# Quarter sums of feed-forward weights: on VectorE, or added in flight by transfers

## What is computed

```python
def _conv_ffn(h, w_up, conv_w, conv_b, w_down):
    up = h @ w_up
    ...
    up = lax.conv_general_dilated(up, rhs, window_strides=(1,), padding=[(CONV_WIDTH - 1, 0)],
                                  dimension_numbers=('NWC', 'WIO', 'NWC'),
                                  feature_group_count=C) + conv_b
    gate, val = up[..., :D_FF], up[..., D_FF:]
    return (jax.nn.silu(gate) * val) @ w_down
```

## Time and profile before

| | us |
|---|---|
| time, median of 3 runs | 1533.74 (1533.73 to 1533.94) |
| profiled execution, its own time | 1533.46 |
| span of the profiled execution | 1531.6 |
| TensorE busy | 1485.4 |
| VectorE busy | 544.0 |
| ScalarE busy | 341.4 |
| GpSimd busy (issuing) | 22.3 |

### The profile page before, as it was taken

How to read it: one execution, slowest core, us unless ns; L and a number is a source line. 1 busy time by engine, 2 the same in 40 slices (tenths; PEclk the granted TensorE clock), 3 DMA queues, 4 the chain that set the end, 5 groups by cost and what they waited for, 6 DMA issues and landing times.

```text
span 1531.6 us, 19436 instructions
## 1 busy us (share of the span) xinstructions
PE 1485.4 (97%) x7522; PEld 841.1 (55%) x7522; DVE 544.0 (36%) x1058; ACT 341.4 (22%) x720; POOL 22.3 (1%) x43
## 2 busy tenths in 40 slices
PE   9999999999999999999989899999989999999997
PEld 8667888999997765444423334433324443433332
DVE  3665665888862343421211121211110212121112
ACT  2443142222223452211101111111101111110112
POOL 0000000000000000000000000000000000000000
PEclk9999999999999999999999999999999999999999
DMA  9735654566652264999999999999999999999996
GB/s 377 290 110 222 248 196 146 214 246 247 268 225 59 79 272 174 391 429 426 430 427 429 429 418 426 428 429 427 429 426 429 413 428 428 426 428 426 427 428 264
DMA packets 46727, 513.61 MB, mean 335 GB/s; under 512 B 5264, under 2 KB 5408, under 8 KB 8384
## 3 DMA queue, kind: packets, MB, share of 16 engines
q1 hardware_dynamic: 41984, 482.53, 76.4%
q0 software_dynamic: 4672, 30.06, 5.1%
HBM read 511.51 MB, written 1.06 MB: 335 GB/s over the span
## 4 chain that ended last, share of the span: by engine, by line
PE 80%; DMA 15%; DVE 2%; ACT 1%; issue 1%; SPq 0%; DVEq 0%; ACTq 0%
PE bank L1452 32%; PE bank L796 13%; DMA ring<-in_gate_w 13%; PE bank L1061 8%; PE bank L1099 5%; PE bank L1416 3%; PE bank L1577 3%; PE bank L1484 3%; PE bank L1300 2%; PE bank L907 2%; DMA ring<-in_down_w 2%; PE bank L1469 2%; PE bank L1253 1%; PE bank L1242 1%; PE bank L1193 1%
## 5 line engine op out<-in xcount | busy, mean ns | idle before, releaser
L1452 PE MATMUL bank<-ring,probs_slab 128*64 128x512 f32 x2824 | 630.6, 596 | 26.6 <-DMA ring<-in_gate_w 15.3
L1452 PEld LDWEIGHTS bank<-ring,probs_slab 128*64 128x64 f32 x2824 | 195.3, 137 | 413.7 <-issue 373.3
L2754 DVE TENSOR_TENSOR squares<-bank,tab 128x512 f32<-128x512 f32 x31 | 21.4, 692 | 465.2 <-PE bank L1469 465.2
L2762 DVE TENSOR_TENSOR squares<-bank,tab 128x512 f32<-128x512 f32 x31 | 21.4, 691 | 180.0 <-PE bank L1469 180.0
L796 PE MATMUL bank<-normed,ring 128*128 128x256 f32 x384 | 84.7, 381 | 0.4 <-ACT normed L1742 0.4
L796 PEld LDWEIGHTS bank<-normed,ring 128*128 128x128 f32 x384 | 72.2, 190 | 11.9 <-ACT normed L1742 1.2
L1099 PE MATMUL bank<-big_slab,ring 128*128 128x256 f32 x352 | 77.6, 380 | 0.0
L1099 PEld LDWEIGHTS bank<-big_slab,ring 128*128 128x128 f32 x352 | 66.3, 191 | 8.4
L2097 ACT ACTIVATE squares<-bank 128x512 f32<-128x512 f32 x31 | 18.5, 597 | 228.1 <-PE bank L1452 228.1
L1416 PEld LDWEIGHTS bank<-tab,residual 128*128 128x128 f32 x512 | 58.4, 192 | 12.9 <-issue 12.9
L2107 ACT ACTIVATE squares<-bank 128x512 f32<-128x512 f32 x30 | 17.9, 597 | 202.4 <-PE bank L1452 202.4
(11 more groups left out here) (426 smaller groups left out, 1612.8 us busy)
## 6 DMA issues: line engine op xcount, KB each, us to landing
ring<-in_down_w SPq DMA_DIRECT2D x61, 2048.0 KB, 17.8
ring<-in_up_w SPq DMA_DIRECT2D x60, 2048.0 KB, 19.5
ring<-in_gate_w SPq DMA_DIRECT2D x58, 2048.0 KB, 19.3
ring<-in_front_w SPq DMA_DIRECT2D x72, 1024.0 KB, 5.0
memory_slab<-in_mod_w POOLq DMA_DIRECT2D x10, 1024.0 KB, 6.6
cross_keys_slab<-in_mod_w POOLq DMA_DIRECT2D x5, 1024.0 KB, 7.9
probs_turned_slab<-in_mod_w POOLq DMA_DIRECT2D x5, 1024.0 KB, 6.9
ring<-in_down_w SPq DMA_DIRECT2D x5, 1024.0 KB, 22.9
```

The source lines that it names most:

```text
L1452: mm = pe.matmul(to[half * SLOTS:(half + 1) * SLOTS, :], tokens(k), weights[:, half * D + i * HALF:half * D + (i + 1) * HALF], start=(k == ...
```

## The change

- t1 and the sum in the ring's slot are no longer formed by VectorE. GpSimd issues three transfers per chunk, each of a quarter (128 x 512, 256 KB) from `front_w` in HBM: a plain copy of quarter (0, 0) into t1, quarter (1, 1) added in flight onto quarter (0, 1) in the ring's slot, and, when the copy has landed, quarter (0, 1) added in flight onto t1. `add_quarters` waits for the products of chunk f - 2 and for the transfers of chunk f - 1 before it begins.
- VectorE forms t2 and t4 alone, after waiting for t1 (`row_sum_here`). Signs differ, since the transfers only add; the merge gets one instruction more (its last one, 128 x 256, becomes two of 128 x 128), and two of the token sums change sign.
- TensorE waits in addition for the sum in the ring's slot (`column_sum_here`).
- On GpSimd's queue the transfers of chunks 2 and 3 stand ahead of `load_mod` 8 to 10. The later `load_mod` are placed after `add_quarters(f + 2)` of the step in which `modulate(n - 3)` is done. They still wait for it.
- Two pairs of semaphores are joined (the two gain rows; the final root), and counts are adapted.

```diff
-WEIGHT_SUMS, MERGES, INPUT_SUMS, _n = {2: 0, 3: 8}, {}, 4, 12
+WEIGHT_SUMS, MERGES, INPUT_SUMS, _n = {2: 0, 3: 6}, {}, 2, 8
...
-            for n in range(DC, MOD_ROUNDS * DC):
+            def late_mod(n):
                 pool.wait_ge(s_mod, mod_steps(max(n - 2, DC)))
                 load_mod(n)
+
+            def add_quarters(f):
+
+                i = SEVEN.index(f)
+                w, slot, here = ff_ring(f)
+                q = f if f < 2 else 2 + 3 * (f // 2 - 1) + f % 2
+                part = lambda k_half, half: weight_part(front_w[FF_FIRST + q], k_half, half)
+                t1 = ff_b[i % 2][0]
+                if i >= 2:
+                    pool.wait_ge(s_ff_up, SEVEN[i - 2] + 1)
+                else:
+                    pool.wait_ge(s_mod, mod_steps(DC))
+                if i:
+                    pool.wait_ge(row_sum_here, 32 * i)
+                    pool.wait_ge(column_sum_here, 16 * i)
+                pool.dma_start(t1, part(0, 0)).then_inc(row_sum_here, 16)
+                pool.wait_ge(chunk_here[slot], here)
+                pool.dma_start(weight_part(w, 0, 1), part(1, 1), accum_op=ADD).then_inc(column_sum_here, 16)
+                pool.wait_ge(row_sum_here, 32 * i + 16)
+                pool.dma_start(t1, part(0, 1), accum_op=ADD).then_inc(row_sum_here, 16)
+
+            add_quarters(2)
+            add_quarters(3)
+            for n in (DC, DC + 1, DC + 2):
+                late_mod(n)
+            used_at = {n: f for f, group in MODULATED_AT.items() for n in group}
+            for f in range(2, FF_CHUNKS):
+                if f + 2 in SEVEN:
+                    add_quarters(f + 2)
+                for n in range(DC + 3, MOD_ROUNDS * DC):
+                    if used_at[n - 3] == f:
+                        late_mod(n)
...
-                pe.wait_ge(s_ff_sums, max(WEIGHT_SUMS[f], INPUT_SUMS) + 4)
+                pe.wait_ge(s_ff_sums, max(WEIGHT_SUMS[f] + 2, INPUT_SUMS + 4))
+                pe.wait_ge(column_sum_here, 16 * (i + 1))
...
-                b00, b10, b01, b11 = [weight_part(w, k_half, half) for half in range(2) for k_half in range(2)]
-                dve.tensor_tensor(t1, b01, b00, SUB).then_inc(s_ff_sums, 1)
+                dve.wait_ge(row_sum_here, 32 * (i + 1))
+                dve.tensor_tensor(t2, weight_part(w, 1, 1), t1, ADD).then_inc(s_ff_sums, 1)
                 dve.wait_ge(s_ff_sums, WEIGHT_SUMS[f] + 1)
-                dve.tensor_tensor(b01, b11, b01, SUB).then_inc(s_ff_sums, 1)
-                dve.tensor_tensor(t2, b11, t1, SUB).then_inc(s_ff_sums, 1)
-                dve.wait_ge(s_ff_sums, WEIGHT_SUMS[f] + 3)
-                dve.tensor_tensor(t4, b10, t2, SUB).then_inc(s_ff_sums, 1)
+                dve.tensor_tensor(t4, weight_part(w, 1, 0), t2, ADD).then_inc(s_ff_sums, 1)
...
                 dve.wait_ge(s_ff_up, f + 1)
-                dve.tensor_tensor(ff_u[i % 2][:, P:3 * P].rearrange("p (c n) -> p c n", c=2),
-                                  bank[2 * ((f + 1) % 2) + 1][:, P:3 * P].rearrange("p (c n) -> p c n", c=2),
-                                  over(six, 2), ADD).then_inc(s_ff_sums, 1)
-                dve.wait_ge(s_ff_sums, MERGES[f] + 4)
+                shared = bank[2 * ((f + 1) % 2) + 1]
+                dve.tensor_tensor(ff_u[i % 2][:, P:2 * P], shared[:, P:2 * P], six, SUB).then_inc(s_ff_sums, 1)
+                dve.tensor_tensor(ff_u[i % 2][:, 2 * P:3 * P], shared[:, 2 * P:3 * P], six, ADD)\
+                    .then_inc(s_ff_sums, 1)
+                dve.wait_ge(s_ff_sums, MERGES[f] + 5)
```

More of the change, by code:

```diff
@@ L120 @@
         MERGES[_f] = _n
-        _n += 4
+        _n += 5
     if _f > 1 and _f + 2 in SEVEN:
         WEIGHT_SUMS[_f + 2] = _n
-        _n += 4
+        _n += 2
 MODULATED_AT = {3: [8, 9], 7: [10, 11], 9: [12], 11: [13, 14], 13: [15, 16], 15: [17, 18], 17: [19, 20], 19: [21, 22],
@@ L359, in build_program @@
                 ("x0", "x1", "par", "mem", "ctx", "tab", "pool", "dft", "moe_tables", "moe_bias", "wr",
-                 "mix_gain", "out_gain")}
+                 "gain_rows")}
         s_sq = sem("squares_ready")
@@ L385, in build_program @@
         s_dve = sem("dve_step")
-        s_root = sem("root_ready")
         s_soft = sem("probs_ready")
@@ L406, in build_program @@
         s_ff_read = sem("ff_seven_product_read")
+        row_sum_here = sem("ff_row_sum_here")
+        column_sum_here = sem("ff_column_sum_here")
         s_gate_v = sem("top_exp_ready")
@@ L748, in _ @@
             full(pool, f"at{LHEADS - 1}1")
-            pool.dma_start(mix_gain, rows[0].partition_broadcast(P)).then_inc(s_in["mix_gain"], 16)
+            pool.dma_start(mix_gain, rows[0].partition_broadcast(P)).then_inc(s_in["gain_rows"], 16)
             pool.wait_ge(s_xnew, 3)
@@ L755, in _ @@
             pool.wait_ge(s_chunk, STASHED.stop)
-            pool.dma_start(out_gain, rows[1].partition_broadcast(P)).then_inc(s_in["out_gain"], 16)
-            pool.wait_ge(s_in["out_gain"], 16)
+            pool.dma_start(out_gain, rows[1].partition_broadcast(P)).then_inc(s_in["gain_rows"], 16)
+            pool.wait_ge(s_in["gain_rows"], 32)
             pool.wait_ge(s_in["wr"], 32)
@@ L1046, in ff_bank_free @@
                 if f - 2 in SEVEN:
-                    pe.wait_ge(s_ff_sums, MERGES[f - 2] + 4)
+                    pe.wait_ge(s_ff_sums, MERGES[f - 2] + 5)
                     pe.wait_ge(s_ff_read, 3 * SEVEN.index(f - 2) + 3)
@@ L1899, in ff_base @@
                 elif f in SEVEN:
-                    act.wait_ge(s_ff_sums, MERGES[f] + 4)
+                    act.wait_ge(s_ff_sums, MERGES[f] + 5)
                 else:
@@ L1919, in read_first @@
                 if i >= 2:
-                    act.wait_ge(s_ff_sums, MERGES[SEVEN[i - 2]] + 4)
+                    act.wait_ge(s_ff_sums, MERGES[SEVEN[i - 2]] + 5)
                 act.activation(ff_read[i % 2][:, 0:P], bank[2 * ((f + 1) % 2)][:, 0:P], ACT.Copy).then_inc(s_ff_read, 1)
@@ L2171, in _ @@
                 act.wait_ge(s_out_base, t + 1)
-                mean_root(71 + 2 * t, 84 + t, 74 + t, s_root)
+                mean_root(71 + 2 * t, 84 + t, 74 + t, s_mix_root)
         @block.vector
@@ L2512, in ff_input_sums @@
                 s1, s2, s3, s4 = ff_a
-                dve.tensor_tensor(s1, token_half(0, 1), token_half(1, 1), ADD).then_inc(s_ff_sums, 1)
+                dve.tensor_tensor(s1, token_half(0, 1), token_half(1, 1), SUB).then_inc(s_ff_sums, 1)
                 dve.tensor_tensor(s3, token_half(0, 0), token_half(0, 1), SUB).then_inc(s_ff_sums, 1)
                 dve.wait_ge(s_ff_sums, INPUT_SUMS + 1)
-                dve.tensor_tensor(s2, s1, token_half(0, 0), SUB).then_inc(s_ff_sums, 1)
+                dve.tensor_tensor(s2, token_half(0, 0), s1, SUB).then_inc(s_ff_sums, 1)
                 dve.wait_ge(s_ff_sums, INPUT_SUMS + 3)
@@ L2523, in ff_merge @@
                 dve.wait_ge(s_ff_read, 3 * i + 2)
-                dve.tensor_tensor(six, six, one, ADD).then_inc(s_ff_sums, 1)
+                dve.tensor_tensor(six, six, one, SUB).then_inc(s_ff_sums, 1)
                 dve.wait_ge(s_ff_sums, MERGES[f] + 1)
-                dve.tensor_tensor(seventh, seventh, six, ADD).then_inc(s_ff_sums, 1)
+                dve.tensor_tensor(seventh, six, seventh, SUB).then_inc(s_ff_sums, 1)
                 dve.wait_ge(s_ff_sums, MERGES[f] + 2)
@@ L2714, in _ @@
             opening_pair = [ranks_of(expert_at(0)), ranks_of(expert_at(1))]
-            dve.wait_ge(s_in["mix_gain"], 16)
+            dve.wait_ge(s_in["gain_rows"], 16)
             mix_gained(0)
@@ L2915, in _ @@
                     up_side(item, e, 0)
-            dve.wait_ge(s_in["out_gain"], 16)
+            dve.wait_ge(s_in["gain_rows"], 32)
             def out_gained(t, half):
@@ L2933, in final @@
             def final(t):
-                step(rstd(74 + t, s_root, t))
+                step(rstd(74 + t, s_mix_root, t + 2))
                 for half in range(2):
```

## The result

The changed kernel takes **1625.65 us** (median of 4 runs, 1623.66 to 1628.64) against 1533.74 (4 runs, 1533.17 to 1533.94): a ratio of 1.060, interval 1.0589 to 1.0615, so 91.9 us slower. Forecast were 50 us, so the loss came as predicted in sign and in kind, and was 1.8 times the size; 1625.65 lies 0.65 us above the range.

A forecast was written before the change was run, and what follows sets the result against it. TensorE was taken to bound the feed-forward, so VectorE's saved 24 us gain 0; 0 + 1.6 (entry) + 48.4 (rounds with loads) = 50 us slower, 1584 us forecast, range 1533 to 1625 us.

The forecast's parts named there:

- R: Moment the second transfer into t1 has landed; allowed at most 8.3 us after the end of chunk f.
- rounds with loads: Feed-forward rounds whose copy queues behind GpSimd's loads: 27.4 us for 19.42 in six steps; with step 9, 48.4 us lost.
- The start: Transfers for chunks 2 and 3, before the feed-forward proper: claimed to cost 0 us, hidden by 15 us of slack.
- step 5: Feed-forward round without loads: claimed to stay about 19.4 us, its transfers hidden.
- How long the transfers take: Prediction's step pricing a 256 KB quarter on GpSimd's queue: copy 3.7 us, adding 4.3 us.
- t: Time for a quarter's plain copy to land: 3.2 us plus 0.5 us mean for meeting ring loads, 3.7 us.
- a: Time for a quarter's adding transfer to land: movement counted twice, 4.3 us, between ends of 2.6 and 9.6 us.
- step 9: Feed-forward round with one load: claimed 21.95 us, 2.5 us over 19.42.
- entry: Beginning of the feed-forward's rounds: chunk 5's R was claimed to come 1.6 us late, a loss of 1.6 us.
- slow adding, over 65 us: Rival that adding transfers are slow: 77 us lost at a = 6, 113 us at a = 8; chance 0.18.
- the copies don't stand behind the loads: Rival that quarters interleave with loads ahead on GpSimd's queue, so everything is hidden: 1534 us; hidden case's chance 0.15.
- Volume is not the limit even if the adding doubles it: Claim on feed-forward DMA traffic: 79 GB/s added beside 236 GB/s, where the expert stage moves 427 GB/s.

The follow-up runs named there:

- e1: Changed kernel with all four weight sums back on VectorE and no quarter transfers, the side edits kept: 1533.41 us, ratio 0.9999 to before.
- e5: Changed kernel with VectorE's products of the conditions placed ahead of the weight sums: 1591.88 us, ratio 1.0391 to before.
- e10: Changed kernel with four buffers for t1 from chunk 4 on and transfers issued for chunk f + 4, still one after another: 1582.41 us.
- e8: e10 with the next chunk's copy issued ahead of this chunk's adding, two semaphores in turn: 1550.99 us, ratio 1.0116 to before.
- e9: e8 with three semaphores for t1 and two for the ring's sum, so nothing waits for the landing of the chunk just before: 1538.08 us.
- e4: Changed kernel with plain copies in place of the two adding transfers, same places and waits: 1608.09 us, ratio 1.0492 to before.
- e3: Changed kernel with only t1 formed by copy and adding transfer, the ring's sum back on VectorE: 1612.58 us, ratio 1.053 to before.
- e6: Changed kernel with the late loads of the conditions' weights issued by ScalarE after its silu, off GpSimd's queue: 1608.33 us, ratio 1.0486 to before.
- e7: Changed kernel with both products of the conditions first on VectorE and late loads issued by ScalarE: 1603.53 us, ratio 1.0474 to before.
- e2: Changed kernel with only the ring slot's sum added in flight, the other three sums back on VectorE: 1533.71 us, ratio 1.0002 to before.
- e11: e9 with the ring's sum back on VectorE, 20 adding transfers fewer: 1533.75 us, ratio 1.0002 to before.

## Why the prediction was right in kind and wrong in size

**What held.** TensorE bounds the stage and VectorE's saved 24 us are worth nothing (e1: putting the work back changes nothing). The side edits cost nothing (e1). The loss comes from transfers that follow one another and from what VectorE does between R and the second load (e5 takes that part out, 34 us; e10, e8 and e9 take out the whole loop, 88 us, and these contain what e5 gives). That the waits would name L2497 and `read_shared`, and that VectorE would wait for `held_slab`, came true, and the rounds with loads were indeed the longer ones. The start cost nothing: those transfers landed by 242 us. The rounds with loads took 27.6 to 33.0 us, the one of step 5, without loads, 25.2.

**The step that failed** is "How long the transfers take": t = 3.7 and a = 4.3 us, where both measured 5.3, and the 0.1 to 0.2 us for the releases, where a chunk has 0.8. Each length built on them failed with it:

| term | forecast | measured in the stage |
|---|---|---|
| copy t, no load ahead | 3.7 | 5.3 |
| adding a | 4.3 | 5.3 |
| from a chunk's landing to the next copy's issue | 0.1 | 0.5 |
| from a copy's landing to the adding's issue | - | 0.3 |
| R to second load's issue, mean of six | 6.1 | 6.1 |
| second load's issue to its landing, mean of six | 8.2 | 6.4 |
| its landing to that of the copy behind it, mean of six | 0.6 | 0.9 |
| round with two loads, mean of six | 27.4 | 30.0 |
| step 9 | 21.95 | 28.8 |
| step 5, no loads | 19.4 | 25.2 |
| entry | 1.6 | 12 |

The first rows carry the others. In a round without loads, 2 (5.3 + 5.3 + 0.8) = 22.8 us, already over 19.42; the forecast had 16.2 and so a step 5 that is hidden, a take-over only at a = 5.9, and an entry of 1.6 us. With t of 5.3 and 0.8 of releases the take-over is at a = 3.6, and every round is in the loop. In the round with loads, 6.1 + 6.4 + 0.9 + 0.3 + 5.3 + 0.5 + 5.3 + 0.3 + 5.3 + 0.1 = 30.5 us, against a measured mean of 30.0. By these the six rounds lost 63.7 us (46 forecast), step 9 9.4 (2.5), step 5 5.8 (0) and the entry 12 (1.6).

The 92 us fall in the branch "slow adding, over 65 us", but not for its reason. Between its cases a = 6 (77 us) and a = 8 (113 us) it takes an a of some 6.8 to lose 92; a was 5.3, and e4, which makes it a copy, gives only 17.6 us back. The copies were as slow as the adding ones.

Three choices lay under it. First, the surcharge for meeting other traffic, which I had at 0.5 us on the mean. The 3.2 us of an unmet quarter was right: the quickest of all 256 KB copies of these runs took 3.26 us (one each in e3 and e4). But in the stage the 18 copies landed after 4.2 to 8.0 us and the 18 adding ones onto t1 after 3.9 to 7.5 us, and e4's copies in their place after 4.6 us on the mean, so traffic costs 1.4 to 2.1 us and not 0.5. The fit of the Trainium skill that the prediction cited (DMA: Bandwidth & Descriptors, Anatomy of one DMA) gives an estimated 2.6 us for a quarter; the measurement stands above it even at its lowest, 3.26. Second, I left GpSimd's own reaction out: a transfer is issued 0.3 us after the landing it waits for, and 0.5 us where it is the next chunk's copy, which waits for more semaphores. Third, in the other direction, I took the second load's 8.2 us from the pairs of before; here it was 6.4. With 6.4 the forecast would have been some 11 us lower, about 39: this error made up by luck for a part of the others.

The rival "the copies don't stand behind the loads" is refuted. A copy issued 0.5 to 0.9 us behind a load never overtook it: in all seven cases it landed 0.64 to 1.38 us after the load. In the round shown above, the load issued at 410.67 and the copy issued at 411.21:

```profile
memory_slab<-in_mod_w POOLq DMA_DIRECT2D x1, 1024.0 KB, 6.1
held_slab<-in_front_w POOLq DMA_DIRECT2D x1, 256.0 KB, 6.2
```

These seven copies took 6.5 us from their own issue, the eleven others 5.3: little more, because the others are met by traffic too.

**"Volume is not the limit even if the adding doubles it"** was judged by the wrong measure, 79 GB/s beside 236 and 427. An adding quarter takes 1.75 us of all 16 engines, 2.8 times what its bytes would at 427 GB/s (0.62 us), and a copy 1.4 times. With all three transfers per chunk the engines' share is 0.92 to 1.03 (e9), and the third transfer costs 4.3 us when nothing else waits, whether by the engines or by its place in the queue. In the changed kernel this didn't show, since the stage had been stretched: 0.76.

**What I didn't see** is the loop through t1's two buffers and TensorE's fallen clock. In the changed kernel it set one copy, that of step 5, and some 0.8 us. But it made e6 and e7 miss: both expected that shortening one loop would pay in full, and the next stood a few us below.

## What to carry to other kernels

Count the links of a loop of transfers first, and price each by its landing time amid the stage's traffic, with the queue's reaction, not by its bytes; a transfer that nothing waits for may take 5 us or 10 and cost nothing (e2, e11), and four in a row cost four times that per round. Give a chain of transfers its lead (buffers) and its overlap (semaphores) before blaming the operation: they were 88 of the 92 us here, and making the adding transfers copies in the old order gave back only 18 (e4). Judge DMA load by the engines' share: where transfers add, GB/s understate it (300 GB/s at a share of 0.98 in e9, 427 at 1.01 in the expert stage of before).

## What the runs showed of the hardware

- A transfer that adds in flight takes twice the DMA engines' time of a copy of the same bytes: 1.68 to 1.75 us for 0.87, at 256 KB. It lands little later: onto t1 after 5.3 us on the mean, the copy in its place (e4) after 4.6. GpSimd issues it in 0.83 to 0.93 us, a copy in 0.54 to 0.57 us (changed kernel).
- Transfers of GpSimd's queue landed in the order of their issue: in the changed kernel's feed-forward none landed before one issued ahead of it, and a 256 KB copy behind a 1024 KB load landed 0.64 to 1.38 us after the load, seven times of seven.
- GpSimd's queue reacts 0.3 us after a landing (0.5 us before a copy, which waits for more semaphores): over the 18 chunks of the stage, at 0.8 us each, an estimate of 14 us.
- Where TensorE waited several us a round, its granted clock fell to 0.84 to 0.96 over 40 us, and pieces ran at the lower of its two levels, 1.2 GHz: 16 records in 3.80 us at a granted clock of 0.50, for 2.07 elsewhere in e6. In e7 48 records took 8.55 us at 0.64, a mixture of both levels, for 5.62. Where it didn't wait it stayed at 1.00.
- At a DMA share of 0.87 to 0.95 (e8) GpSimd's loads of 1024 KB landed after 9.8 us on the mean, in the changed kernel at 0.76 to 0.78 after 5.8. In e2, at 0.68 to 0.88, they landed after some 8 us at no loss of time.
